# Token rows without the norm's weight, and a slot table built in two operations: one edit to a mixture-of-experts kernel

## The reference

```python
u = rmsnorm(h, ffn_norm)                  # h / rms(h) * gain, 1024 wide
g_prob = softmax(u @ wg + bg)             # 8 groups; the best is taken
e_logits = (u @ we + be)                  # 64 experts; the 8 of that group are kept
e_p, e_idx = top_k(softmax(e_logits), 2)  # the two best of them
gates = g_p * e_p / sum(e_p)
# each token goes to its two experts, in 64 of them:
hdn = silu(xb @ w_gate[e]) * (xb @ w_up[e])   # 1024 -> 512
y   = hdn @ w_down[e]                         # 512 -> 1024
out[token] += gate * y
```

## Time and profile before

| | us |
|---|---|
| median of 3 runs | 3245.54 |
| the three runs | 3240.31, 3245.54, 3246.12 |
| profiled execution, its own time | 3237.26 |
| profiled execution, span of its instructions | 3235.4 |
| mean granted clock of TensorE | 0.941 of full speed |
| PE busy | 2729.7 (84% of the span) |
| DVE busy | 1362.6 (42%) |
| POOL busy | 743.6 (23%) |
| ACT busy | 556.1 (17%) |
| DMA | 1043.69 MB, 323 GB/s in the mean |

### The profile page before, as it was taken

One profiled execution on the slowest core, in us unless ns is written; L12 is line 12 of the kernel. 1 busy time (PEld: TensorE's weight loads), 2 busy tenths in 40 slices (PEclk: granted clock), 3 DMA queues, 4 the chain that ended last, 5 costly groups with the idle time before them and its releaser, 6 DMA issues. The chain is left out here.

```text
span 3235.4 us, 27378 instructions
## 1 busy us (share of the span) xinstructions
PE 2729.7 (84%) x9860; PEld 1393.9 (43%) x9860; DVE 1362.6 (42%) x3247; ACT 556.1 (17%) x1348; POOL 743.6 (23%) x626
## 2 busy tenths in 40 slices
PE   6999597788887888659999899999999877777787
PEld 5655233333333333234558756565455433332232
DVE  2152400000000000044523466676766777777774
ACT  2122100000000000012101122222222322222222
POOL 0000100000000000001340134433434444444442
PEclk9999799998899999879999999999999989999999
DMA  3001599999999999531114599999999999999997
GB/s 142 27 20 65 213 407 426 427 427 426 425 421 418 420 419 417 242 127 49 57 52 139 189 419 419 417 417 419 403 418 411 401 416 420 417 414 420 413 407 318
DMA packets 136694, 1043.69 MB, mean 323 GB/s; under 512 B 21792, under 2 KB 22640, under 8 KB 45936
## 3 DMA queue, kind: packets, MB, share of 16 engines
q0 software_dynamic: 82944, 545.32, 41.1%
q1 hardware_dynamic: 53616, 496.63, 37.5%
HBM read 1046.06 MB, written 20.97 MB: 330 GB/s over the span
## 5 line engine op out<-in xcount | busy, mean ns | idle before, releaser
L2137 PE MATMUL psum<-peer_ring,peer_diag 128*128 128x512 f32 x2048 | 972.2, 626 | 194.2 <-ACT peer_diag L2191 193.9
L2006 POOL DMA_INDIRECT peer_ring<-in_peer_uv,peer_pick x512 | 589.0, 1150 | 947.5 <-PE psum L2137 749.5
L2297 DVE CUSTOM_DVE_ANT_0 peer_ring<-peer_ring,sb_rows 128x1024 f32<-128x1024 f32 x512 | 621.5, 1225 | 381.1 <-DMA peer_ring<-in_peer_uv,peer_pick 372.0
L2137 PEld LDWEIGHTS psum<-peer_ring,peer_diag 128*128 128x128 f32 x2048 | 397.0, 199 | 731.6 <-issue 429.8
L1132 PE MATMUL psum<-ffn1w_w,sb_y 128*64 128x512 f32 x2048 | 509.9, 655 | 121.9 <-DMA ffn1w_w<-in_w_up 81.0
L1176 DVE TENSOR_TENSOR sb_y<-psum,sb_y 128x512 f32<-128x512 f32 x32 | 22.1, 692 | 879.8 <-ACT sb_y L1160 879.8
L1132 PEld LDWEIGHTS psum<-ffn1w_w,sb_y 128*64 128x64 f32 x2048 | 180.9, 150 | 449.3 <-issue 447.6
L1153 PE MATMUL psum<-ffn1w_w,moe_hT 128*64 128x512 f32 x1024 | 228.5, 598 | 37.0 <-DVE moe_hT L1181 33.5
L1522 PE MATMUL psum<-sb_y,sb_tiles 128*128 128x512 f32 (+1 forms) x640 | 228.4, 515 | 19.2 <-PEq L104 18.5
L1208 POOL DMA_INDIRECT expert_rows<-sb_tiles,ffn_block_tok x32 | 32.2, 1006 | 897.9 <-ACT sb_tiles L1166 897.9
L2184 ACT ACTIVATE peer_acts<-peer_dots 128x2 f32<-128x2 f32 x256 | 52.1, 203 | 1018.1 <-DVE peer_dots L2297 1018.0
(11 more groups left out here) (412 smaller groups left out, 2299.6 us busy)
## 6 DMA issues: line engine op xcount, KB each, us to landing
ffn1w_w<-in_w_gate SPq DMA_DIRECT2D x64, 2048.0 KB, 28.3
ffn1w_w<-in_w_up SPq DMA_DIRECT2D x64, 2048.0 KB, 28.5
ffn1w_w<-in_w_down SPq DMA_DIRECT2D x64, 2048.0 KB, 29.1
sb_tiles<-in_w_in2b SPq DMA_DIRECT2D x44, 512.0 KB, 3.4
sb_tiles<-in_w_query SPq DMA_DIRECT2D x32, 512.0 KB, 8.0
sb_tiles<-in_w_out SPq DMA_DIRECT2D x24, 512.0 KB, 3.3
sb_tiles<-in_w_br SPq DMA_DIRECT2D x16, 512.0 KB, 5.6
peer_ring<-in_peer_uv,peer_pick POOLq DMA_INDIRECT x512, 13.1
```

The source lines that it names most:

```text
L2006: pool.indirect_dma_start(out=ring[:, slot], out_offset=None, in_=A["peer_uv"], in_offset=bass.IndirectOffsetOnAxis(ap=pick[:, i, j:j + 1] ...
L2137: last = nc.tensor.matmul(ps[:, BANK[i] + c], diag[:, b % DIAGS, x], ring[:, slot, D + 512 * c:D + 512 * (c + 1)], start=False, stop=end, ...
L2297: dve.tensor_tensor_reduce(ring[:, n % RING, 0:D], ring[:, n % RING, 0:D], hr[:, i], 1.0, 0.0, ALU.mult, ALU.add, dots[:, i, j + x:j + x + ...
```

## The change

The gain leaves the token rows. `T_rows` holds rows scaled by 1/rms only, stored by SP as soon as ACT has scaled them; the load of `ffn_rows` and POOL's four multiplications are gone. In exchange `tokens_out` multiplies by the gain as it takes the turned rows out of PSUM; the gain is laid out for that as eight more columns of the small vector `vec`. The 16 instructions of `high` become two, one for the comparison with the block's number and one for the product with the tokens' numbers. The comparison `le` moves from ahead of the table to behind it.

```diff
-              ("lb0", KH), ("lb1", KH), ("conv", 3 * KH)])
+              ("lb0", KH), ("lb1", KH), ("conv", 3 * KH), ("ffn_dims", KD)])
...
-        sl, le = room(1280, [2, NT, N_EXPERTS]), room(1792, [NS, N_EXPERTS])
-        low, high = room(2816, [W, P]), room(1024, [W, NB, 2])
+        sl, le = room(1280, [2, NT, N_EXPERTS]), room(3072, [NS, N_EXPERTS])
+        low, high = room(1792, [W, P]), room(1024, [W, NB, 2])
...
+        in_block = room(0, [W, NB])
...
             def _(sp):
...
-                sp.wait_ge(w_used[3], turns + 2)
-                sp.dma_start(gain_row, A["ffn_rows"]).then_inc(gain_in, 16)
                 for i in range(NT):
-                    sp.wait_ge(row_done, i + 1)
+                    sp.wait_ge(scaled, i + 1)
                     sp.dma_start(T_rows[i * P:(i + 1) * P], rows[:, i]).then_inc(saved, 16)
...
             def _(dve):
...
                 step(dve.tensor_copy(ex[:, NS:NS + 1], nbe[:, N_EXPERTS - 1:N_EXPERTS]))
-                step(dve.tensor_tensor(le, nbe.unsqueeze(1).to_broadcast([P, NS, N_EXPERTS]),
-                                       io[:, 0:NS].unsqueeze(2).to_broadcast([P, NS, N_EXPERTS]), ALU.is_le))
                 step(dve.tensor_tensor(low, io[:].unsqueeze(1).to_broadcast([P, W, P]),
                                        sf[:, 0].unsqueeze(2).to_broadcast([P, W, P]), ALU.is_equal))
-                for o in range(2):
-                    for n in range(W):
-                        last = dve.tensor_scalar(high[:, n, :, o], io[:, 0:NB], sf[:, 1, n:n + 1], tok[:, n, o:o + 1],
-                                                 ALU.is_equal, ALU.mult)
-                step(last)
+                step(dve.tensor_tensor(in_block, io[:, 0:NB].unsqueeze(1).to_broadcast([P, W, NB]),
+                                       sf[:, 1].unsqueeze(2).to_broadcast([P, W, NB]), ALU.is_equal))
+                step(dve.tensor_tensor(high, in_block.unsqueeze(3).to_broadcast([P, W, NB, 2]),
+                                       tok[:].unsqueeze(2).to_broadcast([P, W, NB, 2]), ALU.mult))
                 dve.sem_inc(hot_ready, 1)
...
                 step(dve.tensor_tensor(gates[:, 1], gates[:, 0], ea[:], ALU.mult))
+                step(dve.tensor_tensor(le, nbe.unsqueeze(1).to_broadcast([P, NS, N_EXPERTS]),
+                                       io[:, 0:NS].unsqueeze(2).to_broadcast([P, NS, N_EXPERTS]), ALU.is_le))
                 step(dve.tensor_reduce(ex[:, 0:NS], le, AX.X, ALU.add))
...
             def _(pool):
...
-                pool.wait_ge(gain_in, 16)
-                for i in range(NT):
-                    pool.wait_ge(scaled, i + 1)
-                    pool.tensor_tensor(rows[:, i], rows[:, i], gain_row, ALU.mult).then_inc(row_done, 1)
                 pool.wait_ge(table_ready, 1)
                 pool.wait_ge(saved, 16 * NT)
...
+    gain = core.vec[:, VEC["ffn_dims"]]
...
         def tokens_out(dve, u, n, seen):
             dve.wait_ge(turned, n + 1)
             dve.wait_ge(used[UP], seen)
-            dve.tensor_copy(xT[:, u], ps[:, 0:2].rearrange("p b (k s) -> p (b k) s", s=S2)).then_inc(x_ready, 1)
+            dve.tensor_tensor(xT[:, u], ps[:, 0:2].rearrange("p b (k s) -> p (b k) s", s=S2),
+                              gain.unsqueeze(2).to_broadcast([P, KD, S2]), ALU.mult).then_inc(x_ready, 1)
```

More of the change, by code:

```diff
@@ L834, in route @@
         xg = core.w.tiles[:, 0:2].rearrange("p u k c -> p u (k c)")
-        gain_row = core.w.tiles[:, 3].rearrange("p k c -> p (k c)")
         def room(at, shape):
@@ L848, in route @@
         hot = room(3840, [NT, N_GROUPS])
+        in_block = room(0, [W, NB])
         cnt, nb, nbe, base = (room(2816 + n * N_EXPERTS, [N_EXPERTS]) for n in range(4))
-        (loaded, gain_in, wr_ready, added, chunk_ps, logits_ps, logits_out, lg_ps, squared, folded, row_out, inv_ready,
-         rs_ready, scaled, row_done, saved, own, a_in, a_out, pick_ready, count_ps, rank_ps, hot_ready, table_ps, cleared,
+        (loaded, wr_ready, added, chunk_ps, logits_ps, logits_out, lg_ps, squared, folded, row_out, inv_ready,
+         rs_ready, scaled, saved, own, a_in, a_out, pick_ready, count_ps, rank_ps, hot_ready, table_ps, cleared,
          table_ready) = (st.sem(n) for n in (
-             "ld", "gi", "wr", "added", "chunk", "lgps", "lgout", "lg", "sq", "fold", "ro", "inv",
-             "rs", "scaled", "rd", "sv", "own", "ai", "ao", "pk", "cps", "rk", "hot", "tps", "cl", "table"))
+             "ld", "wr", "added", "chunk", "lgps", "lgout", "lg", "sq", "fold", "ro", "inv",
+             "rs", "scaled", "sv", "own", "ai", "ao", "pk", "cps", "rk", "hot", "tps", "cl", "table"))
         w_tile, w_ready, w_used, turns = core.w.tiles, core.w.ready, core.w.summed, core.w.turns
@@ L2478, in lay_out @@
     a["peer_uv"] = np.concatenate([i["peer_u_2"][0], i["peer_v_2"][0]], axis=1)
-    a["ffn_rows"] = np.broadcast_to(i["ffn_norm"][0], (P, D))
     a["final2_rows"] = np.broadcast_to(i["norm_final_g_2"], (P, D))
@@ L2484, in lay_out @@
             "b_a": i["gla_b_a"][0], "hg_out": i["hg_out_norm_g_2"][0],
-            "lb0": i["hg_lb_logits_2"][0], "lb1": i["hg_lb_logits_2"][1], "conv": i["conv_w_2"][0].reshape(-1)}
+            "lb0": i["hg_lb_logits_2"][0], "lb1": i["hg_lb_logits_2"][1], "conv": i["conv_w_2"][0].reshape(-1),
+            "ffn_dims": i["ffn_norm"][0].reshape(P, KD).T.reshape(-1)}
     a["vectors"] = np.concatenate([_cols(vecs[n]) for n in VEC], axis=1)
```

## The result

The changed kernel takes 3209.72 us (median of 4 runs, 3209.16 to 3210.05) and the kernel before 3245.05 (median of 4). The ratio is 0.9899, with a 95% interval of 0.9886 to 0.9911. By the medians that is 35.3 us less, where 9.8 were forecast. The ratio isn't the quotient of the two medians (which is 0.9891); of 3245.05 us it makes 32.8 us, with bounds of 28.9 and 37.0.

The account below looks back on a forecast made before the run. `experts` was taken as bound by weight loads, whose stream starts only after `route`'s chain through DVE, PE and POOL. Terms 6.4 + 1.25 + 2.1 - 0.01 = 9.8 us off 3245.54 gave 3235.7 us, range 3228 to 3245.

Parts of the forecast that it names:

- The multiplications' removal: In `route`, dropping POOL's four multiplications frees DVE's stalled small instructions: 6.4 us less, or 0 if POOL isn't the cause.
- `le`: In `route`, moved behind the table: 1.25 us off the path, hidden beside POOL's gathers; at worst its whole 1.22 returns.
- `high`: In `route`, 16 instructions become two ahead of PE's table product: 2.1 us less, bounds 1.5 and 2.2.
- The stores: Row stores in `route` move forward to ACT's scaling: cost zero, with 13 us of cover before the gather.
- POOL's drain: At the end of `route`, stays last ahead of the barrier, 6.0 us after the table; DVE's tail ends at 4.1.
- `tokens_out`: In `experts`, multiplying by the gain out of PSUM takes 1.23 us against 1.215 for the copy: +0.01 once.
- The rival in which it makes PE the bound of `experts`: Longer `tokens_out` delays PE's down product: slower by over 6.5 us from 4.2 us growth, 3265 with two stalls; chance 0.04.
- Eight more columns in `vec` cost nothing: The gain's extra columns in the small vector: 4 KB in a load already there, priced at zero.
- follow barrier by barrier: Stages behind `route`: no fixed point in time, so the whole 9.8 us earlier start carries to the end.
- what wasn't thought of: Unnamed causes, counted on the slower side with PE becoming the bound of `experts`; chance 0.04 together.

Follow-up runs that it names:

- e8: Kernel before with only the 16 instructions of `high` made into two: 3241.65 us in one run; `route_total` to first gather 34.4 us, from 36.5.
- e12: Changed kernel with the comparison `le` put back ahead of the table: 3206.12 us in one run; `route_total` to first gather 27.9 us, from 26.7.
- e2: Changed kernel with an unused 32 bytes per partition ahead of `peer`'s ring, which then begins 32 bytes behind a multiple of 512: 3232.42 us, ratio 0.9974.
- e1: Kernel before with an unused 32 bytes per partition ahead of `peer`'s ring, which then begins at byte 92160 as in the changed kernel: 3216.38 us, ratio 0.992.
- e7: Changed kernel with POOL again doing four 128 x 1024 multiplications, into a tile nobody reads, stores still early: 3213.61 us in one run.

## Why the prediction was wrong

**The sum was right.** The multiplications' removal was priced at 6.4 us, `le` at 1.25, `high` at 2.1: 9.8. The profile gives 36.5 - 26.7 = 9.8 for the stretch, e8 gives 2.1 for `high`, e12 gives 1.2 for `le`, which leaves 6.5 for the multiplications; and e2, the change with the ring off the grain, gives 10.3 us of total time by the medians, 8.4 by the ratio (3232.42 from 3242.70; the forecast was 3235.7 from 3245.54).

**What was hidden stayed hidden.** The stores were issued at 359.61 to 363.34. SP's wait for them ended at about 369.6, 14 us ahead of the gather. `le`, at 383.62, ran beside POOL's issues of 1.16 and 0.99 us, which were 1.18 and 0.98 before: nothing was held. POOL's drain, from 383.7 to 388.3, remained the last thing ahead of the barrier; DVE was done at 386.51. `tokens_out` took 1.215 us as the copy did:

```profile
L1165 DVE TENSOR_TENSOR sb_y<-psum,sb_vec x32: 1212/1215/1225, 390.7 to 1318.0; 128x1024 f32<-128x1024 f32 x32
```

The rival in which it makes PE the bound of `experts` therefore never came near its threshold of 4.0 us of growth; the stretch is 977.2 beside 976.8.

**The step that failed** is one sentence of the sum: "Eight more columns in `vec` cost nothing: 4 KB in a load that is already there." I priced the eight columns as data and not as space. They moved every tensor that is allocated behind `vec` by 32 bytes, and with them the landing place of the 512 x 128 x 8 KB = 537 MB that `peer` gathers, from 224 bytes behind a multiple of 256 onto one. That is worth 23.0 us in the profile, and 26.3 of total time by e1's median. Whether the place sets the rate at all was a question that the prediction never asked; that it fell on a good place was luck. The next sentence that leaned on it, that later stages only "follow barrier by barrier", was true up to the first product of `peer` (493.9 and 493.6 us) and false from there. Of the rivals none had the right sign and size, since all of them looked for what the edit does to instructions and waits, and what wasn't thought of had its 0.04 on the slower side. The range, 3228 to 3245, was as narrow as the spread of one mechanism. Nothing in a trace shows an address, so the 418 GB/s of the kernel before looked like a ceiling of the DMA rather than a loss; what could have raised the question is the stream of `experts`, which the same trace shows at 426 GB/s from 500 to 900 us, 2% above the stream of `peer`. It would have raised it only: later in the same stage, with the ring where it was, the slices read 417 to 421, and no run here says why.

## What to carry to other kernels

A change in the size of a tensor that is allocated early moves everything behind it, unless the allocator's rounding absorbs it. When a stage streams rows of some KB (8 here) into SBUF at a DMA share of 1.0, look where the rows land, put that tensor on a multiple of 256 bytes on purpose, and hold its place fixed when you measure another edit, or the measurement is of both. And where one engine's small instructions take ten times their usual duration, look for the other engine's long one that ends at the same moment.

## What the runs showed of the hardware

**The place of a DMA's target in SBUF.** Gathers of 8 KB rows into a tensor that begins on a multiple of 256 bytes run at 424 to 426 GB/s from 1900 to 2200 us. At 32, 64, 128 or 224 bytes behind one they run at 416 to 419. The six places tried agree on a grain of 256. The Trainium skill, page "DMA: Bandwidth & Descriptors", section "How a descriptor splits into AXI transactions", says that a descriptor is split into transactions of 256 bytes which start at multiples of 256; one of 576 bytes takes three where it starts on such a multiple, and four where it starts at byte 224. By that rule, as an estimate, an 8 KB row off the grain takes 33 in place of 32, which is 3.1% more; 1.7% was measured. The page speaks of reads, and here it is the written side that was moved. That this splitting is the mechanism is therefore an inference; the grain and the size are shown.

**A stall of DVE beside POOL, by its length.** In e7 DVE's first stalled instruction took 1.74 us in place of 2.22 when POOL's instruction took 1.95 in place of 2.31 (it started 0.18 and 0.15 us behind POOL's): what is held waits for the end of what holds it.

**A spread that comes from the first 300 us.** `route_total` starts at 351.1 to 352.6 us in six profiles and at 355.8 to 356.7 in eight, in kernels with the same work up to there, and with the ring on the grain or off it in either group. The kernel before is at 351.3 and e1, whose only edit lies far behind, at 356.1. Between the profiles of before and after 1.5 us of the 5.4 arise before 27 us, and 3.0 between 278 and 297 us. In that stretch the granted clock of the changed kernel is 0.50 from 286 to 292 us (the level of 1.2 GHz) and that of the kernel before 1.00. In the 6 us ahead of it, from 280 to 286, PE was busy for 5.08 us in the first and 4.92 in the second, at 0.95 and 1.00. Six microseconds at half the clock are worth about 3, an estimate which fits. Why the clock fell in one execution and not in the other stays open. A span can differ by this much with no cause in the edit.
